# Constant products in front of 25 TensorE waits, a token-wise final norm and a reordered recurrent mixer in a two-model fp32 kernel

## What is computed

```python
def reference(...):
    x = first_block(...)            # 2 layers: modulated norm, one wide projection, a convolution
                                    # branch, neighbourhood attention, window attention, merge
    return second_block(x, ...)

def second_block(x, ...):
    h = x
    for layer in range(2):
        h = h + (rglru_mixer if layer == 0 else nsa_mixer)(rmsnorm(h, ...), ...)
        h = h + conv_ffn(rmsnorm(h, ...), ...)
    return rmsnorm(h, final_norm_g)

def rmsnorm(x, g):
    return x * rsqrt(mean(x * x, axis=-1) + EPS) * g

def rglru_mixer(x, ...):            # y_br = gelu(x @ w[:, :1280]), x_br = x @ w[:, 1280:]
    xc = causal_dwconv(x_br)
    r, i = sigmoid(blockwise(xc))   # 10 blocks of 128 channels
    a = exp(-8 * r * softplus(-a_param)); b = sqrt(1 - a * a) * i * xc
    return (scan(a, b) * y_br) @ w_out
```

## Time and profile before

| what | value |
|---|---|
| median of three runs | 3262.49 us (3261.21 to 3264.74) |
| the profiled execution: its time | 3261.86 us |
| its span, first to last instruction | 3260.0 us |
| mean granted TensorE clock | 0.974 |
| TensorE busy (products) | 3074.2 us, 94% |
| VectorE, ScalarE, GpSimd busy | 57%, 40%, 10% |

### The profile page before, as it was taken

One profiled execution on the slowest core, in us unless ns is written; L12 is line 12 of the kernel. 1 busy time (PEld: TensorE's weight loads), 2 busy tenths in 40 slices (PEclk: granted clock), 3 DMA queues, 4 the chain that ended last, 5 costly groups with the idle time before them and its releaser, 6 DMA issues. The chain is left out here.

```text
span 3260.0 us, 36655 instructions
## 1 busy us (share of the span) xinstructions
PE 3074.2 (94%) x14600; PEld 2414.3 (74%) x14600; DVE 1856.7 (57%) x2911; ACT 1305.8 (40%) x2017; POOL 337.2 (10%) x237
## 2 busy tenths in 40 slices
PE   8989999989999988899899999999999889999998
PEld 5877777877788676668666777788887766788886
DVE  5867695454434667674533786666435662466633
ACT  3344534234432344533444465322225556422221
POOL 0011231210000001101220021000003210000000
PEclk9999999999999999999999999999999999999998
DMA  5222132320012322223111332333332310223331
GB/s 206 69 61 72 46 117 77 107 77 27 20 33 67 109 78 78 65 81 97 38 30 42 91 101 80 96 97 94 94 96 81 110 36 1 71 91 97 96 94 63
DMA packets 78731, 251.49 MB, mean 77 GB/s; under 512 B 9120, under 2 KB 11168, under 8 KB 78560
## 3 DMA queue, kind: packets, MB, share of 16 engines
q1 hardware_dynamic: 72672, 227.91, 22.6%
q0 software_dynamic: 5024, 18.09, 1.8%
q10 hardware_dynamic: 864, 3.15, 0.2%
HBM read 247.01 MB, written 2.10 MB: 76 GB/s over the span
## 5 line engine op out<-in xcount | busy, mean ns | idle before, releaser
L1049 DVE TENSOR_TENSOR WL<-RAW,WH 128x1024 fp32r<-128x1024 f32 (+3 forms) x372 | 429.3, 1155 | 516.2 <-ACT WH L1039 515.5
L1039 ACT ACTIVATE WH<-RAW 128x1024 fp32r<-128x1024 f32 (+4 forms) x425 | 407.7, 965 | 425.5 <-PE PS L1090 325.7
L1630 PE MATMUL PS<-Hh,WH 128*128 128x512 f32 x1376 | 526.6, 383 | 19.9 <-DVE WL L1049 7.8
L1630 PE MATMUL PS<-Hl,WH 128*128 128x512 f32 x1376 | 497.0, 361 | 0.0
L1630 PE MATMUL PS<-Hh,WL 128*128 128x512 f32 x1376 | 496.6, 361 | 0.0
L1630 PEld LDWEIGHTS PS<-Hh,WH 128*128 128x128 f32 x1376 | 267.5, 194 | 83.2 <-issue 30.5
L1090 PE MATMUL PS<-XH,WH 128*128 128x512 f32 x768 | 306.1, 399 | 0.0
L1090 PE MATMUL PS<-XH,WL 128*128 128x512 f32 x768 | 304.4, 396 | 0.0
L1090 PE MATMUL PS<-XL,WH 128*128 128x512 f32 x768 | 304.4, 396 | 0.0
L1630 PEld LDWEIGHTS PS<-Hl,WH 128*128 128x128 f32 x1376 | 267.1, 194 | 46.3 <-issue 7.7
L1630 PEld LDWEIGHTS PS<-Hh,WL 128*128 128x128 f32 x1376 | 267.3, 194 | 39.9
(11 more groups left out here) (385 smaller groups left out, 5697.2 us busy)
## 6 DMA issues: line engine op xcount, KB each, us to landing
RAW<-in_w_in SPq DMA_DIRECT2D x124, 512.0 KB, 3.6
RAW<-in_ffn_in SPq DMA_DIRECT2D x96, 512.0 KB, 3.6
RAW<-in_ffn_out SPq DMA_DIRECT2D x48, 512.0 KB, 3.5
RAW<-in_w_ada SPq DMA_DIRECT2D x32, 384.0 KB, 3.5
RAW<-in_nsa_in SPq DMA_DIRECT2D x21, 512.0 KB, 3.2
RAW<-in_lru_in SPq DMA_DIRECT2D x20, 512.0 KB, 3.7
MW<-in_w_ada SPq DMA_DIRECT2D x32, 256.0 KB, 9.7
BS<-in_bs POOLq DMA_DIRECT2D x16, 512.0 KB, 3.9
```

What stands on the lines that cost most here:

```text
L1039: act.activation(WH[half[j]][:, 0:n], RAW[j % NRAW][:, 0:n], ACT.Copy).then_inc(*did("act_whi", ("whi", j)))
L1049: dve.tensor_tensor(WL[half[j]][:, 0:n], RAW[j % NRAW][:, 0:n], WH[half[j]][:, 0:n].bitcast(F32), ALU.subtract).then_inc(*did("dve_wlo", ( ...
L1630: mm = pe.matmul(ps[:, c:c + w_], wt[:, 128 * k:128 * k + 128], x[:, a:a + w_], start=(k == 0 and q == 0), stop=(k == n - 1 and q == 2))
```

## The change

Three edits.

**Constant products.** A table KEEP names 21 steps of the four attention orders and a count for each; KEEP_OWN names four linears or modulation steps. In front of the step TensorE makes that many products of the identity with 256 columns of a constant tile, in full fp32, into columns 768 to 1023 of the PSUM pair of the linear that is open (or is about to be), which nobody reads. They are 118 in all, in 25 places, and wait for nothing in 21 of them; in the four of KEEP_OWN for the pair alone.

```diff
+KEEP = {
+    ('vt', ('av', 0, 0, 0)): 7,
+    ('max', 0, 0, 0, 0, 3): 9,
+    ('st', 0, 0, 0, 0, 3): 3,
...
+    ('pv', 1, 1, 2, 0, 0): 2,
+    ('pv', 1, 1, 3, 0, 0): 6,
+}
+KEEP_OWN = {
+    ('pj', 0, 0, 0): 7,
+    ('modt', 2): 3,
+    ('pj', 1, 0, 0): 7,
+    ('mg', 1, 0, 7): 5,
+}
...
+        def pe_keep(pe, n):
+            if n:
+                dst = spare["part"]
+            for _ in range(n):
+                pe.matmul(dst, ident, CO[:, 0:256], start=False, stop=False, skip_group_check=True)
...
+            if k == 0 and nm in KEEP_OWN:
+                for w in due("pe", pairs.after[nm], ("co",)):
+                    pe.wait_ge(*w)
+                spare["part"] = ps[:, 768:1024]
+                pe_keep(pe, KEEP_OWN[nm])
             for w in due("pe", ("wlo", j), pairs.after[nm], need):
                 pe.wait_ge(*w)
+            spare["part"] = ps[:, 768:1024] if k < n - 1 else None
...
             for u in P.orders[L, br]:
+                pe_keep(pe, KEEP.get(u, 0))
```

```diff
-        in_turn([self.recur(m) for m in range(10)])
+        in_turn([self.recur(m) for m in range(10)] + [self.second(0)])
...
                 if m - 1 in FRONT:
                     act_mult(act, SCANS[FRONT[m - 1]])
+                    act_split(act, ahead(nm) + 1)
...
                 if m - 1 in FRONT:
                     dve_tall(dve, SCANS[FRONT[m - 1]])
+                if m:
+                    dve_low(dve, m - 1)
...
-                for i in LOWS[m]:
-                    for w in due("dve", ("lgh", i), ("rym", i)):
-                        dve.wait_ge(*w)
-                    dve.tensor_tensor(LGl[:, i, :], buf((("ry", i), "g"))[:, 0:S], LGh[:, i, :].bitcast(F32), ALU.subtract).then_inc(*did("dve_g", ("lgl", i)))
+            dve_low(dve, 9)
```

```diff
                 pe_linear(pe, ("ao", sq, m), src, R512, need)
-                if m == 7:
+                if m == 7 and sq in NEXT:
                     pe_square(pe, sq, 6)
-            if sq not in NEXT:
-                pe_square(pe, sq, 7)
+                if m and sq == LAST:
+                    pe_turned(pe, m - 1)
...
+            for i in range(4):
+                pe.matmul(sums[:, i:i + 1], early[:, 128 * i:128 * i + 128], ones[:, 0:1], start=True, stop=False)
+                mm = pe.matmul(sums[:, i:i + 1], late[:, 128 * i:128 * i + 128], ones[:, 0:1], start=False, stop=True)
+            mm.then_inc(*did("pe_sq", ("sqm", LAST, 7)))
+            pe_turned(pe, 7)
...
+            for i, c0, n in ((1, 0, 1024), (3, 512, 512)):
...
+                act.activation(OU[:, i, c0:c0 + n], OU[:, i, c0:c0 + n], ACT.Copy, scale=ROOT[:, i:i + 1]).then_inc(*did("act_ou", ("ou", i)))
...
+            for i, n in ((0, 1024), (2, 1024), (3, 512)):
...
+                dve.tensor_scalar(OU[:, i, 0:n], OU[:, i, 0:n], ROOT[:, i:i + 1], None, ALU.mult).then_inc(*did("dve_ou", ("ou", i)))
```

More of the change, by code:

```diff
@@ L251, in __init__ @@
         sq = self.ffn(1, sq)
[L252 to L255, removed]
     def chunk(self, name, part, args):
@@ L666, in recur, with second @@
         self.tmp.release((nm, "xc"), ("i1", m))
+    def second(self, m):
+        nm = ("ry", m)
+        self.linear(nm, [(("lru_in", m, 0, 1024, 1), list(range(8)))])
+        self.tmp.take((nm, "g"))
+        self.pairs.release(nm, (nm, "g"))
+        yield
     def lru(self):
@@ L670, in lru @@
         self.root_held(sq)
-        in_turn([self.recur(m) for m in range(10)])
+        in_turn([self.recur(m) for m in range(10)] + [self.second(0)])
         for m in range(10):
[L673 to L676, removed]
+            if m:
+                next(self.second(m))
             for i in LOWS[m]:
@@ L945, in build @@
             PTN = [sb(f"PTN{i}", [128, 512], F32, p2) for i in range(4)]
+        with ExitStack() as p2:
+            OU = sb("OU", [128, 4, 1024], F32, p2)
         XH, XL = (sb(x, [128, 8, S], F32R) for x in ("XH", "XL"))
@@ L1437, in pe_tick @@
                 pe.wait_ge(*w)
+            spare["part"] = ps[:, 768:1024] if 0 <= c and k < 7 else None
             for q, wt in enumerate((RAW[j % NRAW],) if whole else (WH[half[j]], WL[half[j]])):
@@ L2253, in act_next @@
             act_square(act, sq, m, ("x2", sq, m))
+            if sq == LAST:
+                y = buf(("fy", m))[:, 0:S]
+                for w in due("act", ("x2", sq, m), was(("fy", m))):
+                    act.wait_ge(*w)
+                act.activation(y, X[:, m, 0:S], ACT.Identity, scale=sm("final_g", m, 1)).then_inc(*did("act_fy", ("fy", m)))
         def dve_add_out(dve, sq):
@@ L2475, in dve_lru, with dve_low @@
                 dve.wait_ge(*w)
+        def dve_low(dve, m):
+            for i in LOWS[m]:
+                for w in due("dve", ("lgh", i), ("rym", i)):
+                    dve.wait_ge(*w)
+                dve.tensor_tensor(LGl[:, i, :], buf((("ry", i), "g"))[:, 0:S], LGh[:, i, :].bitcast(F32), ALU.subtract).then_inc(*did("dve_g", ("lgl", i)))
         def dve_taken(dve, m):
@@ new lines, in pe_end @@
+                mm = pe.matmul(sums[:, i:i + 1], late[:, 128 * i:128 * i + 128], ones[:, 0:1], start=False, stop=True)
+            mm.then_inc(*did("pe_sq", ("sqm", LAST, 7)))
+            pe_turned(pe, 7)
+        def act_end(act):
+            for w in due("act", ("end", 0)):
+                act.wait_ge(*w)
+            act.activation(ROOT, FULL, ACT.Ln).then_inc(*did("act_rs", ("end", 1)))
+            for w in due("act", ("end", 1)):
+                act.wait_ge(*w)
+            act.activation(ROOT, ROOT, ACT.Exp, scale=-0.5).then_inc(*did("act_rs", ("end", 2)))
+            for i, c0, n in ((1, 0, 1024), (3, 512, 512)):
+                for w in due("act", ("end", 5), [("fe", m) for m in range(8)]):
@@ L3043, in dve_end @@
-            for i in range(4):
-                for w in due("dve", ("ot2", i), ("stored", i - 2) if i >= 2 else None):
-                    dve.wait_ge(*w)
-                dve.tensor_copy(OU[i % 2][:, 0:512], pairs.of(("out", i))[:, 0:512]).then_inc(*did("dve_ou", ("ou", i)))
+            for w in due("dve", ("sqm", LAST, 7)):
+                dve.wait_ge(*w)
+            dve.tensor_scalar(FULL, pairs.of(("sq", LAST))[:, 0:4], 1.0 / 1024, EPS, ALU.mult, ALU.add).then_inc(*did("dve_rs", ("end", 0)))
```

96 lines of the change are left out of this document (70 added, 26 removed).

## The result

The changed kernel takes 3225.19 us (median of four runs, 3222.85 to 3228.23), the kernel before 3262.32 us beside it. The ratio is 0.9882, with a 95% interval of 0.987 to 0.9894: faster by 37 us. The forecast was 3222 us, so it lies 3.2 us off. The profiled execution took 3228.23 us, the slowest of the four, and its span is 3226.4 us.

What follows compares the result with a forecast made beforehand. The prediction took TensorE, its waits and its half-clock stretches, to bound the kernel. Constant products -30, mixer -1.5 and token norm -9.1 sum to -40.6 us, from 3262.5 to 3222 us, range 3205 to 3243.

Steps and rivals of the forecast that it cites:

- What bounds the kernel: Whole kernel: TensorE is busy for 94% of the span; the question is where it waits or runs at half clock.
- The fills cost nothing: Attention: 118 constant products, 49.6 us, fit inside 72.2 us of waits, leaving at least 0.5 us idle each time.
- What they bring: Attention stretch: constant products keep TensorE at full clock, -30 us, between -42 and -9.
- three falls at 1.75: Attention stretch: three new clock falls at gaps the table leaves uncovered, each costing 1.75 us.
- I take four fifths: Attention stretch: of the 42 us by which TensorE's work shrinks, 33.5 us pass on.
- The identity and the clock: Fills: were products with the identity treated like transposes, not counted as activity, the constant products' term would be 0.
- The mixer: Recurrent mixer: moving `ry 0` ahead of `gw 8` covers the first wait; -1.5 us, between -6.5 and +2.
- the last three LGl: Mixer's end: made until 1997.0 by DVE; the output linear needs them 1.2 us later, cutting the gain to about 1.2.
- The token norm: Kernel's end: 14.6 us in place of 23.7, -9.1 us, between -11 and -6.
- The rival of moving falls: Attention: waits grow past the fills, the clock falls there or at other gaps; 12 us remain, 3240 us, chance 0.13.
- The others: Rivals: faster in full, 3205 us (0.10); products do not hold the clock, 3252 (0.06); fills overrun, slower, 3279 (0.04).
- What would show it: Right: clock about 0.99, 8 to 14 half-clock stretches, idle 0.5 to 1.5 us; wrong: over 4 us before `ry 7`, late output linear.

Runs made afterwards that it cites:

- double_fill: The changed kernel with the mixer's old order and every fill twice as long, 236 products in the 25 places; 3235.75 us, ratio 0.9921.
- keep_only: The kernel before with the 118 constant products alone, mixer and end as before; 3226.18 us, ratio 0.9888.
- turned_fill: The changed kernel with the mixer's old order and the fills at twelve places of layer 1 made as transposes against the identity; 3221.63 us, ratio 0.9877.
- mixer_only: The kernel before with the reordered recurrent mixer alone; 3265.71 us, ratio 1.001.

## Why the prediction was right, point by point

**What bounds the kernel**: right. All that the first edit brings comes from TensorE's clock.

**The fills cost nothing**: right. The idle left is 0.39 to 1.08 us; 0.5 at least was forecast, and two places are just under it (0.39 and 0.49). None overruns. `double_fill` shows the price once the cover is gone: 24.7 us over the 25 places.

**What they bring**: the term was -30 us between -42 and -9; `keep_only` gives -37.2, inside the range and 7 us better. By its own parts the term is -28.3 (33.5 less three falls at 1.75), so -30 holds a slip of 1.7 us. The step that was mis-sized is "I take four fifths". In front of the mixer the work at half clock fell by 98.5 us in `keep_only` (116.7 to 18.2), which is more than the 94.2 us at the places alone, and at 44% it is 43.3 us; the idle time fell by 46.4 us against some 50 of fills. That makes 39.7 us, and 36.8 were measured. So nearly all of the shorter work passed on: the ACT and DVE chains moved forward with TensorE. In the kernel after, the lead is 34.6 us at the mixer's start, with just the three new falls in the attention that were forecast; one of them, though, came where no wait over 0.6 us stood. Less the 5.5 us of falls in the sparse attention it is 29 us. That this matches the -30 is partly luck: the share passed on was taken too low, and the falls in a stage 800 us later, which has no fills, were not counted at all.

**The identity and the clock**: right. By the Trainium skill (TensorE: Matmul & The Clock Gate, part 4, PE-mode transpose) a transpose does not count as activity; the timing beside that rule is of bf16, the transposes here are fp32. The trace of `turned_fill` disagrees: with twelve fills made of transposes the clock is 0.99 in their 600 us, and there are no more falls than with products. The measurement decides here.

**The mixer**: wrong in sign. The term was -1.5 us between -6.5 and +2; `mixer_only` is +2.3 slower, and +3.3 in its profiled run, past the upper end. Its first steps held: `ry 0` covers the first wait, and a wait of 3.48 us stands before `ry 7` (3.9 forecast). The step that failed is "the last three LGl ... the output linear needs them 1.2 us later than that". That looked only at the last three. The LGl of the blocks before are also behind WL now, and TensorE waits for two of them inside the first group of the output linear, 2.8 us. The three short waits for the weights of `ry 5`, `ry 8` and `ry 9`, 2.4 us together, were not in the forecast either. It gave no price to what the new turns put beside GpSimd. The kernel after has, in DVE's and then GpSimd's timeline:

```profile
1919.10 1.23 DVE L1095 TENSOR_TENSOR WL<-RAW,WH 128x1024 fp32r<-128x1024 f32 x1 [0.74 <-ACT WH L1085]
...
1923.78 2.30 DVE L1095 TENSOR_TENSOR WL<-RAW,WH 128x1024 fp32r<-128x1024 f32 x1
...
1938.83 1.77 DVE L2559 TENSOR_TENSOR LGl<-U,LGh 128x512 fp32r<-128x512 f32 x1
...
1942.22 2.32 DVE L1095 TENSOR_TENSOR WL<-RAW,WH 128x1024 fp32r<-128x1024 f32 x1
1944.46 0.68 DVE L2559 TENSOR_TENSOR LGl<-U,LGh 128x512 fp32r<-128x512 f32 x1
```

```profile
1923.25 1.74 POOL L2602 TENSOR_TENSOR IG<-IG,TH 128x512 f32<-128x512 f32 x1
1924.96 2.28 POOL L2602 TENSOR_TENSOR IG<-IG,TH 128x512 f32<-128x512 f32 x1
...
1938.32 1.73 POOL L2602 TENSOR_TENSOR IG<-IG,TH 128x512 f32<-128x512 f32 x1
...
1941.70 1.75 POOL L2602 TENSOR_TENSOR IG<-IG,TH 128x512 f32<-128x512 f32 x1
```

The two long WL and the long LGl each begin while a product of GpSimd runs; the WL of 1.23 us and the LGl of 0.68 do not. Both long WL end 1.09 us after that product's end (1924.99 to 1926.08, 1943.45 to 1944.54), the LGl 0.55 us after (1940.05 to 1940.60): they stand until GpSimd is done. In the kernel before, no WL of this chain began within such a product. That GpSimd is what holds them is read from these times; no run took GpSimd's products away.

**The token norm**: right, 1 us too hopeful. The term was -9.1, measured -8.1. The transposes: 2.4 us forecast, 2.6 measured. To the scale factors: 4.9 and 5.1. From there to the end: 7.3 and 7.8, and the transfers bind, as taken. The end of the kernel before was taken at its window's length.

**The sum and the rivals.** -40.6 forecast, -37.1 measured. The errors have opposite signs: the fills gave more, the mixer 5 us less, the sparse attention took back 5.5. Without the slip of 1.7 us the sum would be -38.9. The rival of moving falls (3240 us) was right in one half, the new falls at other gaps, and wrong in the other: no wait became shorter than its fill, and behind the 25 places the clock held. The others are out: the mixer lost in place of gaining, the fills hold the clock, and they overrun nowhere.

**What would show it**: 13 stretches (8 to 14 forecast), clock 0.989, 236 records. The two signs of a wrong mixer term were named, a wait before `ry 7` and a late output linear. The second came, while the wait, 3.48 us, stayed under the 4 us that I had set for it. The idle left, 0.39 to 1.08 us, began lower than the 0.5 named.

## What to carry to other kernels

Where the busiest engine waits a few microseconds and its clock falls behind the wait, products that nobody reads are free as long as they end before the wait does; read the rest of the wait at each place, for beyond it they cost time (doubled, 15.9 us here). No free PSUM column is needed, since a product of zeros can go into an open sum. Cover every wait of that length in the program or expect the clock to fall at those left over; a few falls stay even where no wait over 0.8 us stands. When an edit shifts the later stages, their falls lie otherwise, and a difference of 5 us between two versions may be nothing else. Where two engines slow each other, look at which instruction begins within one of the other's before turns are changed. Before one operation is moved past another on a full engine, list all that stand behind it, not the last ones alone.

## What the runs showed of the hardware that was not expected

- Products of zeros hold TensorE's clock like others: 0.99 in the stretch with them, 0.92 without.
- The clock also falls with hardly a wait in front: in the kernel after at 746.9 us, with no wait over 0.6 us in the 9 us before, and in `turned_fill` at 1640.3 us, with none over 0.8.
- Waits of the same length, 1.67 to 2.98 us, are followed by four stretches at half clock in one execution (13.6 us) and by six in another (30.6 us), with the same instructions; one of them lasted 10.2 us, though TensorE was busy throughout it.
- A WL of 128x1024 on DVE takes 1.23 us in the mixer, and 1.85 to 2.32 us where it begins within a GpSimd product of two SBUF tiles. By the Trainium skill (SBUF — State Buffer, Terms, shared port pair) one of the two is locked out for the whole instruction of the other. The trace agrees: in the kernel after 18 WL of this size take over 1.3 us on DVE, and all 18 end 1.08 or 1.09 us after the GpSimd instruction within which they began. The other way round, GpSimd's product begun at 1924.96 us ends 1.16 us after the WL beside it and takes 2.28 us; the shortest of its kind in the mixer takes 1.29. The records overlap, so that of the engine that stands holds its waiting too.
